# Moving the low halves of twenty weight units from GpSimd to VectorE, and reordering the work around them

## The chip, the cores and the metric

The kernel runs on one NeuronCore of a Trainium2 chip. The metric is the device time of one execution in microseconds; the median of several runs counts. The engines are called as the profile calls them: PE (TensorE), DVE (VectorE), ACT (ScalarE), POOL (GpSimd) and SP (SyncE, which issues the DMAs).

## What is computed

The reference is a two-layer transformer backbone over 512 latent tokens and 256 context tokens of width 1024. What matters here is the MLP behind each attention layer, its modulated input and its gated output:

```python
def squared_relu_mlp(h, w_in, w_out):
    return jnp.square(jax.nn.relu(h @ w_in)) @ w_out
...
    ml = jnp.split((c_act @ w_mod[i] + b_mod[i])[:, None, :], 6, axis=-1)
    ...
    xl = xl + ml[5] * squared_relu_mlp(modulate(xl, norm_mlp_g[i], ml[3], ml[4]), w_mlp_in[i], w_mlp_out[i])
    if not last:
        ...
        xc = xc + mc[5] * squared_relu_mlp(modulate(xc, norm_mlp_g[i], mc[3], mc[4]), w_mlp_in[i], w_mlp_out[i])
```

`w_in` is 1024 x 4096 and `w_out` 4096 x 1024, all in float32. The first MLP works on all 768 tokens, the second on the 512 latent ones.

## The kernel before

**Three matmuls for one.** Every operand of a float32 product is split into a high half (`w_hi`, `h_hi`, `hidh`: the value rounded to the matmul's format) and a low half (what is left: `w_lo`, `h_lo`, `hidl`). A product is three matmuls, lines 2109 to 2111: low by high, high by low, high by high.

**Weight units.** The weights come from DRAM in units of 128 x 1024, by SP, into four `raw` slots. For each unit ACT writes the high half (`high_u`, line 949, or `high_sum`, line 964) and POOL the low half in four pieces of 256 columns (`low`, line 744, `w_lo <- raw, w_hi`). PE waits for `lo_made`, a count of finished units in their order; SP reloads a raw slot when the low half that frees it is made (`FREED`).

**The first MLP.** It goes through the 4096 hidden columns in 8 blocks of 512. Block 0 is computed directly. Blocks 1 to 7 split both operands in 2 x 2 parts and use seven products p0 to p6 instead of eight (24 PE matmuls of 384 tokens each), with sums of parts as operands. For the weights, POOL's `summed` (line 770) makes four sums a block: S1 `w_sum = a21 + a22`, S2 `a21 = a11 - a21`, S3 `a11 = w_sum - a11`, S4 `w_sum = a12 - a11`. Products 1 and 3 use S1 and S4 from the one `w_sum` buffer, product 2 uses S3, product 4 uses S2. For the tokens DVE makes t1 to t4 once, at the end of block 0 (`differ`, `join`, `less`), ACT their high halves (`turn_high`, line 971) and DVE their low halves (`turn_low`, line 1681). POOL may start S1 of block 1 when the first `turn_low` is done, because t1 and `w_sum` share memory.

After its seven products, a block's hidden values are finished in quarters on ACT and DVE (`copy`, line 1007, which takes product 0, 1 or 2 out of PSUM; `joined`, line 1768; `quarter_high`, lines 1015 to 1019; `low(q)`, line 1773). PE product 2 waits for the first `copy`; in ACT's queue this copy stands behind `high_sum(b, 3)`, which needs S4. Then PE does the second matrix (`second`): four units of 48 matmuls, two output tiles a unit; the first two column chunks of tile 0 and 1 need quarters 0 and 1, the third chunk needs quarters 2 and 3. DVE adds each finished tile onto the residual (`add_tile`, line 1660).

**Modulation.** DVE also computes late rows of the modulation product (`mod_step`, line 1439, eight steps a row group, fed by SP through a ring of four slots; then `acc_hi`, `acc_lo`), PE sums them over the partitions (`mod_mm`, lines 2150 and 2151), and DVE reads the result out (`extract_late`). Groups 10 and 11 of these fall in the second MLP's first pass: eight units for the hidden values (i = 0 to 7), eight for the output (i = 8 to 15).

Every engine runs its own list in program order; the order is written out by hand.

Of the kernel before, what the change touches and what calls it, by code (L numbers as in the profile page):

```python
# [58 lines left out]
MOD_LATE = {6: (10, (4, 5)), 7: (10, (6, 7)), 8: (11, (0, 1)), 9: (11, (2, 3)), 11: (11, range(4, 8))}  # L59
# [15 lines left out]
def _sources():  # L75

    src, freed = {}, {}
    for b in range(BLOCKS):
        w, r = block_first(b), block_raw(b)
        n = 8 if b == 0 else 0  # L80
        if b:
            src.update({w: r, w + 1: None, w + 2: r, w + 3: None, w + 4: r + 1, w + 5: r + 2, w + 6: r + 3})
            freed.update({r: w + 2, r + 1: w + 4, r + 2: w + 5, r + 3: w + 6})
            w, r, n = w + 7, r + 4, 4 if b < 6 else 0
        for i in range(n):
            src[w + i], freed[r + i] = r + i, w + i
    for i in range(8):
        src[LAST_W + i], freed[LAST_R + i] = LAST_R + i, LAST_W + i
    return src, freed
# [40 lines left out]
def build(nc, t):  # L130

    ctx = ExitStack()
    with ctx:
# [200 lines left out]
        tf_made = sem("tf_made")  # L334
        t_hi = sem("t_hi")
# [400 lines left out]
        def _(pool):  # L736
# [28 lines left out]
            def first_mlp():  # L765
# [9 lines left out]
                for b in range(1, BLOCKS):  # L775
                    w, r, n = M0 + block_first(b), M0 + block_raw(b), 4 * (b - 1)
                    a11, a21, a12, a22 = (raw[:, (r + j) % SLOTS] for j in range(4))

                    def raw_here(j):
                        pool.wait_ge(raw_in[(r + j) % SLOTS], 16 * ((r + j) // SLOTS + 1))  # L780

                    def outer_sums():
                        raw_here(1)
                        raw_here(3)
                        if b == 1:
                            pool.wait_ge(t_lo, 1)
                        else:
                            pool.wait_ge(lo_made, M0 + block_first(b - 1) + 4)
                        summed(w_sum, a21, a22, ALU.add)
                        raw_here(0)  # L790
                        pool.wait_ge(w_sums, n + 1)
                        summed(a21, a11, a21, ALU.subtract)

                    if b < 7:
                        outer_sums()
                    low(w, 4)
                    pool.wait_ge(w_sums, n + 2)
                    pool.wait_ge(lo_made, w + 1)
                    summed(a11, w_sum, a11, ALU.subtract)
                    low(w + 1, 4)  # L800
                    raw_here(2)
                    pool.wait_ge(w_sums, n + 3)
                    pool.wait_ge(lo_made, w + 2)
                    summed(w_sum, a12, a11, ALU.subtract)
                    for j in range(2, 11 if b < 6 else 7):
                        low(w + j, 4)
# [136 lines left out]
        def _(act):  # L943
# [23 lines left out]
            def first_mlp():  # L967

                def turn_high(j, dst, src):
                    act.wait_ge(tf_made, (2, 3, 2, 4)[j])  # L970
                    nc.scalar.activation(dst, src, ACT.Copy).then_inc(t_hi, 1)
# [22 lines left out]
                turn_high(3, t4h[:], t4f[:])  # L994
# [6 lines left out]
                next_block(1)  # L1001
                for b in range(1, BLOCKS):
# [421 lines left out]
        def _(dve):  # L1424
# [252 lines left out]
            def first_mlp():  # L1677
# [8 lines left out]
                def differ(dst, spare, j0, tok0, j1, tok1):  # L1686
                    tt(dst, half_f(j0, 0, tok0), half_f(j1, 0, tok1), op=ALU.subtract).then_inc(dsteps, 1)
                    st.n = st.n + 1
                    st.wait(tt(spare, half_f(j0, 1, tok0), half_f(j1, 1, tok1), op=ALU.subtract))

                def join(dst, other):
# [16 lines left out]
                join(t1f[:], t4f[:])  # L1708
# [33 lines left out]
                join(t3f[:], t4f[:])  # L1742
                add_tile(0, 1)
                less(t2f[:], t1f[:], 1, 1, H1)
                join(t2f[:], half_f(1, 1, H1))
                add_tile(0, 2)
                turn_low(0, h_lo[:, 0:4, H1], t1f[:], h_hi[:, 0:4, H1])
# [10 lines left out]
                for b in range(1, BLOCKS):  # L1758
# [15 lines left out]

                    early = 4 if b < 5 else 6
# [8 lines left out]
                    low(1)  # L1784
                    if b == 6:
                        extract_late(c, 4)
                    joined(1, 5, 2)
                    low(2)
                    low(3)
                    if b < 5:  # L1790
                        for m in range(8):
                            add_tile(b, m)
                            if m < 2:
                                steps(c, range(6 + m, 7 + m))
                            if m == 4:
                                extract_late(c, 0)
                    elif b == 5:
                        add_tile(b, 0)
                        add_tile(b, 1)
                        extract_late(c, 0)  # L1800
# [20 lines left out]
            def mlp():  # L1821
                u0 = FIRST["mlp1"]

                def blk(b, first, last):
                    for i in range(12 if last else 16):
# [3 lines left out]
                        else:  # L1829
                            if first and i in (8, 12):  # L1830
                                dve.wait_ge(mod_done, PE_MODS + i // 4 + 9)
# [3 lines left out]
                        if first:  # L1835
# [3 lines left out]
                            elif i == 7:  # L1839
                                extract_late(10, 6)  # L1840
                            elif i in (8, 9):
                                for k in range(4 * i - 32, 4 * i - 28):
                                    mod_step(11, k)
                            elif i == 10:
                                extract_late(11, 6)
# [258 lines left out]
        def _(pe):  # L2104
# [269 lines left out]
            def mlp(layer=1):  # L2374
# [3 lines left out]
                def blk(b, first, last):  # L2378
                    for i in range(12 if last else 16):
# [24 lines left out]
                        if first and i in (7, 10):  # L2404
                            mod_mm(10 if i == 7 else 11, 6)
# [574 lines left out]
```

## Time and profile before

| | us |
|---|---|
| median of 3 runs | 1601.85 (1601.6 to 1603.73) |
| profiled execution, its own time | 1603.09 |
| its span, first to last instruction | 1601.3 |
| PE busy / DVE busy / ACT busy / POOL busy | 1573.3 / 894.1 / 604.7 / 910.0 |
| PE's longest wait in the first MLP | 4.6, for POOL's `w_lo` |

The busy times are sums over the whole span. A product starts on PE only when the last of its weights, tokens and PSUM banks is there, so a wait of PE names the one that came last, and the row of that engine shows what it waited for in turn.

### The profile page before, as it was taken

The numbers are of one execution on the slowest core, as the hardware profiler recorded it, in microseconds if no ns is written. First come the engines' busy times: TensorE is split into PE (matmuls) and PEld (weight loads), VectorE is DVE, ScalarE is ACT, GpSimd is POOL, SyncE is SP. The second block draws the span as 40 slices with busy tenths as digits, with TensorE's granted clock in tenths as the row PEclk, the third lists the DMA queues.
The fourth block names the chain that finished last, engine by engine and source line by source line (L and its number), as shares of the span: only waits on it lengthen the run. The fifth ranks groups of instructions, "written<-read, shape, count | busy, mean of one in ns | idle before, by whom it ended". The sixth has DMA issues, their size and how long they took to land.

```text
span 1601.3 us, 24059 instructions
## 1 busy us (share of the span) xinstructions
PE 1573.3 (98%) x9272; PEld 1408.7 (88%) x9272; DVE 894.1 (56%) x1364; ACT 604.7 (38%) x1009; POOL 910.0 (57%) x1103
## 2 busy tenths in 40 slices
PE   8999999999899999999999999999999999999998
PEld 5889988988899999999998888878889878888887
DVE  4696457347845656647556746049965753232234
ACT  4422456325252342442542511248853412222222
POOL 2443475326677768768762656354415865555562
PEclk9999999999999999999999999999999999999999
DMA  8574212212042232333352223110003332323221
GB/s 350 197 268 153 93 41 100 80 48 85 27 157 81 80 119 82 116 115 123 105 182 82 91 78 96 66 43 1 1 12 130 129 126 93 105 92 101 83 93 53
DMA packets 50348, 163.15 MB, mean 102 GB/s; under 512 B 6336, under 2 KB 8768, under 8 KB 46656
## 3 DMA queue, kind: packets, MB, share of 16 engines
q1 hardware_dynamic: 50240, 161.68, 29.4%
q8 instruction: 71, 1.16, 0.3%
q14 instruction: 37, 0.30, 0.1%
HBM read 158.78 MB, written 2.10 MB: 100 GB/s over the span
## 4 chain that ended last, share of the span: by engine, by line
PE 86%; DVE 6%; POOL 2%; issue 2%; DMA 2%; ACT 1%; SPq 0%; POOLq 0%; DVEq 0%; ACTq 0%
PE ps L2109 24%; PE ps L2110 24%; PE ps L2111 24%; PE ps L2748 3%; PE ps L2710 2%; PE ps L2737 1%; PE ps L2615 1%; POOL w_lo L744 1%; PE ps L2603 1%; PE ps L2643 1%; PE ps L2427 1%; DVE mod_acc L1439 1%; DMA mod_big<-w_mod_dram 1%; DVE h L1562 1%; DMA raw<-units_dram 1%
## 5 line engine op out<-in xcount | busy, mean ns | idle before, releaser
L744 POOL TENSOR_TENSOR w_lo<-raw,w_hi 128x256 fp32r<-128x256 f32 x776 | 639.4, 856 | 492.4 <-ACT w_hi L949 362.0
L2109 PE MATMUL ps<-h,w_hi 128*128 128x512 f32 (+2 forms) x1016 | 358.0, 352 | 7.2 <-POOL w_lo L744 4.6
L2110 PE MATMUL ps<-h,w_lo 128*128 128x512 f32 (+2 forms) x1016 | 355.3, 350 | 0.0
L2111 PE MATMUL ps<-h,w_hi 128*128 128x512 f32 (+2 forms) x1016 | 355.0, 349 | 0.0
L2109 PEld LDWEIGHTS ps<-h,w_hi 128*128 128x128 f32 x1016 | 192.2, 189 | 32.3 <-issue 9.1
L2111 PEld LDWEIGHTS ps<-h,w_hi 128*128 128x128 f32 x1016 | 192.0, 189 | 17.1
L2110 PEld LDWEIGHTS ps<-h,w_lo 128*128 128x128 f32 x1016 | 192.2, 189 | 16.4
L1660 DVE SCALAR_TENSOR_TENSOR xl<-ps,mods,xl 128x384 f32<-128x384 f32 (+2 forms) x144 | 73.0, 539 | 210.8 <-PE ps L2111 209.0
L949 ACT ACTIVATE w_hi<-raw 128x1024 fp32r<-128x1024 f32 x120 | 126.4, 1054 | 113.2 <-PE ps L2111 107.7
L2109 PE MATMUL ps<-hidl,w_hi 128*128 128x384 f32 (+2 forms) x448 | 150.4, 336 | 2.5 <-DVE hidl L1704 1.5
L2110 PE MATMUL ps<-hidh,w_lo 128*128 128x384 f32 (+2 forms) x448 | 149.8, 334 | 0.0
L2111 PE MATMUL ps<-hidh,w_hi 128*128 128x384 f32 (+2 forms) x448 | 149.8, 334 | 0.0
L1439 DVE SCALAR_TENSOR_TENSOR mod_acc<-mod_ring,cact,mod_acc 128x512 f32<-128x512 f32 x112 | 105.7, 964 | 17.1 <-DVE mod_acc L1439 8.4
L2109 PE MATMUL ps<-hid_lo,w_hi 128*128 128x512 f32 (+1 forms) x288 | 105.6, 367 | 0.8 <-DVE hid_lo L1674 0.8
L2110 PE MATMUL ps<-hid_hi,w_lo 128*128 128x512 f32 (+1 forms) x288 | 105.3, 366 | 0.0
L2111 PE MATMUL ps<-hid_hi,w_hi 128*128 128x512 f32 (+1 forms) x288 | 105.3, 366 | 0.0
L956 ACT ACTIVATE w_hi<-raw 128x1024 fp32r<-128x1024 f32 x60 | 63.4, 1057 | 108.5 <-PE ps L2111 108.5
L2109 PEld LDWEIGHTS ps<-hidl,w_hi 128*128 128x128 f32 x448 | 84.1, 188 | 4.3 <-DVE hidl L1704 1.8
L2110 PEld LDWEIGHTS ps<-hidh,w_lo 128*128 128x128 f32 x448 | 84.1, 188 | 1.3 <-issue 0.2
L2111 PEld LDWEIGHTS ps<-hidh,w_hi 128*128 128x128 f32 x448 | 84.1, 188 | 0.6
L1670 DVE TENSOR_TENSOR tmp_b<-tmp_a 128x512 f32<-128x512 f32 x32 | 28.0, 875 | 81.7 <-ACT tmp_a L1141 81.1
L770 POOL TENSOR_TENSOR w_sum<-raw 128x256 f32<-128x256 f32 x52 | 48.6, 965 | 26.2 <-issue 17.9
(301 smaller groups left out, 3181.1 us busy)
## 6 DMA issues: line engine op xcount, KB each, us to landing
raw<-units_dram SPq DMA_DIRECT2D x187, 512.0 KB, 3.4
mod_ring<-w_mod_dram SPq DMA_DIRECT2D x96, 256.0 KB, 3.9
mod_big<-w_mod_dram SPq DMA_DIRECT2D x16, 1024.0 KB, 10.2
mod_late<-w_mod_dram SPq DMA_DIRECT2D x8, 1024.0 KB, 8.1
xl<-x_dram SPq DMA_DIRECT2D x2, 2048.0 KB, 8.3
bias<-bias_dram SPq DMA_DIRECT2D x8, 384.0 KB, 3.7
xc<-ctx_dram SPq DMA_DIRECT2D x2, 1024.0 KB, 10.4
out_dram<-out_t SPq DMA_DIRECT2D x16, 128.0 KB, 1.8
```

Source lines behind the costliest of these rows:

```text
L744: ins = nc.gpsimd.tensor_tensor(w_lo[:, s, sl], src[:, sl], w_hi[:, s, sl].bitcast(F32), op=ALU.subtract)
L770: ins = nc.gpsimd.tensor_tensor(dst[:, sl], a[:, sl], b[:, sl], op=op)
L949: nc.scalar.activation(w_hi[:, u % SLOTS], raw[:, r % SLOTS], ACT.Copy).then_inc(hi_made, 1)
L956: nc.scalar.activation(w_hi[:, u % SLOTS], raw[:, r % SLOTS], ACT.Copy).then_inc(hi_made, 1)
L1439: ins = V.scalar_tensor_tensor(out=mod_acc[:, v], in0=w, scalar=cact[:, k, v:v + 1], in1=mod_acc[:, v], op0=ALU.mult, op1=ALU.add)
L1660: ins = V.scalar_tensor_tensor(out=x, in0=ps[:, 2 * par + bank, cols], scalar=gate(layer, m, v, i), in1=x, op0=ALU.mult, op1=ALU.add)
L1670: ins = tt(tmp_b[:, i % 2, 0:n], tmp_a[:, i % 2, 0:n], tmp_a[:, i % 2, 0:n], op=ALU.mult)
L2109: mm(out, a[0], b[1], start=start, stop=False, skip_group_check=onto)
L2110: mm(out, a[1], b[0], start=False, stop=False, skip_group_check=onto)
L2111: return mm(out, a[0], b[0], start=False, stop=stop, skip_group_check=onto)
L2710: return mm(scores_ps(n)[:, TOK * i + keys.start:TOK * i + keys.stop], a[p][64 * i:64 * i + 64, tok], b[p][64 * i:64 * i + 64, keys], star ...
L2748: ins = mm(out_ps, v1[:, c, P * h:P * h + P], aturn[m % 2][:, c], start=c == 0, stop=c == NT - 1)
```

## The change

Three things change.

1. At the end of block 0, DVE and ACT take their steps in another order: the low half of t1 comes second instead of after the other sums, ACT's `turn_high(0)` waits for the first join alone (and for a new count `t_read`, that the parts it overwrites were read), and ACT's high half of t4 stands behind the first three weight high halves of block 1.
2. In blocks 1 to 7, POOL makes the low half of product 2's weights before S4 instead of behind it. In blocks 1 to 5 the low halves of the four second-matrix units are made by DVE (`weight_low`), whole units of 1024 columns, between its other steps.
3. In the second MLP's first pass, PE sums group 10 after unit 8 instead of after unit 7 and group 11 after unit 11 instead of after unit 10; DVE reads them out at i = 8 and 12; the steps of group 11 are spread over i = 8, 9, 10 as 2, 3, 3 instead of 4, 4; the ring loads move with them.

```diff
-MOD_LATE = {6: (10, (4, 5)), 7: (10, (6, 7)), 8: (11, (0, 1)), 9: (11, (2, 3)), 11: (11, range(4, 8))}
+MOD_LATE = {6: (10, (4, 5)), 7: (10, (6, 7)), 8: (11, range(4)), 12: (11, range(4, 8))}
...
-            freed.update({r: w + 2, r + 1: w + 4, r + 2: w + 5, r + 3: w + 6})
+            freed.update({r: w + 3, r + 1: w + 4, r + 2: w + 5, r + 3: w + 6})
...
                     low(w + 1, 4)
+                    low(w + 2, 4)
                     raw_here(2)
                     pool.wait_ge(w_sums, n + 3)
                     pool.wait_ge(lo_made, w + 2)
                     summed(w_sum, a12, a11, ALU.subtract)
-                    for j in range(2, 11 if b < 6 else 7):
+                    for j in range(3, 7):
                         low(w + j, 4)
...
-                    act.wait_ge(tf_made, (2, 3, 2, 4)[j])
+                    act.wait_ge(tf_made, (1, 3, 2, 4)[j])
+                    if j == 0:
+                        act.wait_ge(t_read, 4)
...
-                turn_high(3, t4h[:], t4f[:])
...
                 next_block(1)
+                turn_high(3, t4h[:], t4f[:])
...
+                    def weight_low(j):
+                        if b < 6:
+                            u = M0 + block_first(b) + 7 + j
+                            dve.wait_ge(hi_made, u + 1)
+                            dve.wait_ge(lo_made, u)
+                            tt(w_lo[:, u % SLOTS], raw[:, raw_of(u) % SLOTS], w_hi[:, u % SLOTS].bitcast(F32),
+                               op=ALU.subtract).then_inc(lo_made, 1)
...
                     low(1)
+                    weight_low(0)
...
                     joined(1, 5, 2)
                     low(2)
+                    weight_low(1)
                     low(3)
+                    weight_low(2)
...
                             if first and i in (8, 12):
+                                extract_late(i // 4 + 8, 6)
...
-                        if first and i in (7, 10):
-                            mod_mm(10 if i == 7 else 11, 6)
+                        if first and i in (8, 11):
+                            mod_mm(10 if i == 8 else 11, 6)
```

The fourth `weight_low` of a block follows the last modulation step of the row group behind the second `add_tile` (in block 5, the second `add_tile` itself).

POOL's list from the end of block 6 to the end of the first MLP. `w_lo<-w_sum` are the low halves for products 1 and 3, `raw<-w_sum,raw` is S3, `w_sum<-raw` is S4. Before:

```order
L744 TENSOR_TENSOR w_lo<-raw,w_hi 128x256 x16
L770 TENSOR_TENSOR raw<-w_sum,raw 128x256 x4
L744 TENSOR_TENSOR w_lo<-w_sum,w_hi 128x256 x4
L770 TENSOR_TENSOR w_sum<-raw 128x256 x4
L744 TENSOR_TENSOR w_lo<-raw,w_hi 128x256 x4
L744 TENSOR_TENSOR w_lo<-w_sum,w_hi 128x256 x4
L744 TENSOR_TENSOR w_lo<-raw,w_hi 128x256 x60
```

Now:

```order
L745 TENSOR_TENSOR w_lo<-raw,w_hi 128x256 x16
L771 TENSOR_TENSOR raw<-w_sum,raw 128x256 x4
L745 TENSOR_TENSOR w_lo<-w_sum,w_hi 128x256 x4
L745 TENSOR_TENSOR w_lo<-raw,w_hi 128x256 x4
L771 TENSOR_TENSOR w_sum<-raw 128x256 x4
L745 TENSOR_TENSOR w_lo<-w_sum,w_hi 128x256 x4
L745 TENSOR_TENSOR w_lo<-raw,w_hi 128x256 x60
```

S4 of block 7 moved behind the low half of product 2's weights; in blocks 1 to 6 the same pair is swapped.

DVE's list at the end of block 1's products, from the low half of quarter 0 to the first output tile. `hidl<-ps,hidh` are the quarters' low halves, `ps<-ps,hidl_f` are the joins. Before:

```order
L1773 TENSOR_TENSOR hidl<-ps,hidh 128x2x384
L1768 TENSOR_TENSOR ps<-ps,hidl_f 128x2x384
L1439 SCALAR_TENSOR_TENSOR mod_acc<-mod_ring,cact,mod_acc 128x512 x2
L1773 TENSOR_TENSOR hidl<-ps,hidh 128x2x384
L1768 TENSOR_TENSOR ps<-ps,hidl_f 128x2x384
L1773 TENSOR_TENSOR hidl<-ps,hidh 128x2x384 x2
L1660 SCALAR_TENSOR_TENSOR xl<-ps,mods,xl 128x384
```

Now:

```order
L1778 TENSOR_TENSOR hidl<-ps,hidh 128x2x384
L1773 TENSOR_TENSOR ps<-ps,hidl_f 128x2x384
L1443 SCALAR_TENSOR_TENSOR mod_acc<-mod_ring,cact,mod_acc 128x512 x2
L1778 TENSOR_TENSOR hidl<-ps,hidh 128x2x384
L1785 TENSOR_TENSOR w_lo<-raw,w_hi 128x1024
L1773 TENSOR_TENSOR ps<-ps,hidl_f 128x2x384
L1778 TENSOR_TENSOR hidl<-ps,hidh 128x2x384
L1785 TENSOR_TENSOR w_lo<-raw,w_hi 128x1024
L1778 TENSOR_TENSOR hidl<-ps,hidh 128x2x384
L1785 TENSOR_TENSOR w_lo<-raw,w_hi 128x1024
L1664 SCALAR_TENSOR_TENSOR xl<-ps,mods,xl 128x384
```

Three whole-unit low halves now stand between the quarters, the first of them ahead of quarter 2's join.

ACT's list from the last hidden tile of block 0 to block 1's first copy (`hidl_f<-ps`). Before:

```order
L983 ACTIVATE hidh<-hidl_f 128x768
L971 ACTIVATE h<-t1f 128x4x384
L971 ACTIVATE t2h<-t2f 128x1536
L971 ACTIVATE t3h<-t3f 128x1536
L971 ACTIVATE t4h<-t4f 128x1536
L949 ACTIVATE w_hi<-raw 128x1024
L964 ACTIVATE w_hi<-w_sum 128x1024
L964 ACTIVATE w_hi<-raw 128x1024
L964 ACTIVATE w_hi<-w_sum 128x1024
L1007 ACTIVATE hidl_f<-ps 128x2x384
```

Now:

```order
L987 ACTIVATE hidh<-hidl_f 128x768
L975 ACTIVATE h<-t1f 128x4x384
L975 ACTIVATE t2h<-t2f 128x1536
L975 ACTIVATE t3h<-t3f 128x1536
L951 ACTIVATE w_hi<-raw 128x1024
L966 ACTIVATE w_hi<-w_sum 128x1024
L966 ACTIVATE w_hi<-raw 128x1024
L975 ACTIVATE t4h<-t4f 128x1536
L966 ACTIVATE w_hi<-w_sum 128x1024
L1011 ACTIVATE hidl_f<-ps 128x2x384
```

The high half of t4 moved behind the high halves for products 0, 1 and 2.

## Rows read from the trace of the kernel before

**Rows 1.** The page: the span, and PE's busy time, share and instructions.

```profile
span 1601.3 us, 24059 instructions
...
PE 1573.3 (98%) x9272; PEld 1408.7 (88%) x9272; DVE 894.1 (56%) x1364; ACT 604.7 (38%) x1009; POOL 910.0 (57%) x1103
```

**Rows 2.** Waits of PE in the first MLP: total, times, longest.

```profile
PE ps L2109 <- POOL w_lo L744: 4.6, 1, 4.6
```

**Rows 3.** Timeline of PE in block 1: start, duration, instruction, idle before.

```profile
433.40 0.34 PE L2111 MATMUL ps<-h,w_hi 128*128 128x384 f32 x1
...
438.31 0.66 PE L2109 MATMUL ps<-h,w_hi 128*128 128x384 f32 x1 [4.56 <-POOL w_lo L744]
...
445.26 0.34 PE L2109 MATMUL ps<-t2l,w_hi 128*128 128x384 f32 x1
```

**Rows 4.** Windows: length, busy PE PEld DVE ACT POOL, PEclk, DMA.

```profile
437.40:444.20 6.80, 5.89 (x18) 5.93 (x19) 3.37 (x4) 1.90 (x3) 6.63 (x8) 0.50 0.00 0
...
500.30:563.66 63.36, 63.36 (x365) 63.18 (x365) 37.35 (x54) 22.84 (x26) 47.62 (x60) 1.00 0.30 100
```

**Rows 5.** Timeline of POOL from block 0 into block 1.

```profile
385.05 20.75 POOL L744 TENSOR_TENSOR w_lo<-raw,w_hi 128x256 fp32r<-128x256 f32 x16 [7.14 <-ACT w_hi L949]
412.85 4.33 POOL L770 TENSOR_TENSOR w_sum<-raw 128x256 f32<-128x256 f32 x4 [7.05 <-DVE h L1681]
...
426.41 2.83 POOL L744 TENSOR_TENSOR w_lo<-raw,w_hi 128x256 fp32r<-128x256 f32 x4 [4.67 <-ACT w_hi L949]
429.38 4.52 POOL L770 TENSOR_TENSOR raw<-w_sum,raw 128x256 f32<-128x256 f32 x4
```

**Rows 6.** Timeline of DVE and ACT in the same stretch.

```profile
410.93 1.75 DVE L1681 TENSOR_TENSOR h<-t1f,h 128x1536 fp32r<-128x1536 f32 x1
...
425.29 1.04 ACT L949 ACTIVATE w_hi<-raw 128x1024 fp32r<-128x1024 f32 x1
...
443.26 0.79 ACT L1007 ACTIVATE hidl_f<-ps 128x768 f32<-128x768 f32 x1
```

**Rows 7.** Timeline of DVE (low half of quarter 3, third output tile) and PE, block 2.

```profile
532.70 0.96 DVE L1773 TENSOR_TENSOR hidl<-ps,hidh 128x768 fp32r<-128x768 f32 x1 [2.37 <-ACT hidh L1019]
...
544.48 0.86 DVE L1660 SCALAR_TENSOR_TENSOR xl<-ps,mods,xl 128x384 f32<-128x384 f32 x2
...
534.62 0.33 PE L2109 MATMUL ps<-hidl,w_hi 128*128 128x384 f32 x1
```

**Rows 8.** Timeline of DVE, block 6.

```profile
779.00 1.21 DVE L1725 TENSOR_TENSOR w_sum<-raw 128x1024 f32<-128x1024 f32 x1
```

**Rows 9.** Timeline of POOL, start of block 3.

```profile
540.16 4.99 POOL L770 TENSOR_TENSOR w_sum<-raw 128x256 f32<-128x256 f32 x4 [3.66 <-issue]
...
565.06 3.64 POOL L744 TENSOR_TENSOR w_lo<-w_sum,w_hi 128x256 fp32r<-128x256 f32 x4 [2.63 <-ACT w_hi L964]
```

**Rows 10.** Timeline of POOL, ACT and PE, start of block 7.

```profile
787.32 2.82 POOL L770 TENSOR_TENSOR w_sum<-raw 128x256 f32<-128x256 f32 x4 [0.17 <-POOL w_lo L744]
790.10 3.02 POOL L744 TENSOR_TENSOR w_lo<-raw,w_hi 128x256 fp32r<-128x256 f32 x4
...
787.67 1.05 ACT L964 ACTIVATE w_hi<-raw 128x1024 fp32r<-128x1024 f32 x1
...
790.99 1.05 ACT L964 ACTIVATE w_hi<-w_sum 128x1024 fp32r<-128x1024 f32 x1
...
793.17 0.45 PE L2109 MATMUL ps<-t2l,w_hi 128*128 128x384 f32 x1
```

**Rows 11.** Timeline of PE, behind block 7.

```profile
820.95 0.44 PE L2109 MATMUL ps<-h,w_hi 128*128 128x384 f32 x1 [0.43 <-DVE h L1773]
```

**Rows 12.** Timeline of PE, second MLP, first pass.

```profile
1280.39 0.47 PE L2150 MATMUL ps<-acc_lo,ones 128*128 128x512 f32 x1 [1.23 <-DVE acc_lo L1449]
...
1286.64 0.50 PE L2109 MATMUL ps<-hid_lo,w_hi 128*128 128x512 f32 x1 [0.76 <-DVE hid_lo L1674]
...
1299.72 0.48 PE L2150 MATMUL ps<-acc_lo,ones 128*128 128x512 f32 x1 [1.19 <-DVE acc_lo L1449]
```

More of the change, by code:

```diff
@@ L334, in build @@
         tf_made = sem("tf_made")
+        t_read = sem("t_read")
         t_hi = sem("t_hi")
@@ L1686, in differ, with join @@
                 def differ(dst, spare, j0, tok0, j1, tok1):
[L1687 to L1691, printed above, removed]
+                    tt(dst, half_f(j0, 0, tok0), half_f(j1, 0, tok1), op=ALU.subtract).then_inc(t_read, 1)
+                    tt(spare, half_f(j0, 1, tok0), half_f(j1, 1, tok1), op=ALU.subtract).then_inc(t_read, 1)
+                def join(dst, other, reads=None):
+                    if reads:
+                        dve.wait_ge(t_read, reads)
                     tt(dst, dst, other, op=ALU.add).then_inc(tf_made, 1)
@@ L1707, in first_mlp @@
                 differ(t1f[:], t4f[:], 0, H1, 0, H0)
-                join(t1f[:], t4f[:])
+                join(t1f[:], t4f[:], 2)
                 first_square(0)
@@ L1741, in first_mlp @@
                 add_tile(0, 0)
-                join(t3f[:], t4f[:])
+                less(t2f[:], t1f[:], 1, 1, H1)
+                turn_low(0, h_lo[:, 0:4, H1], t1f[:], h_hi[:, 0:4, H1])
                 add_tile(0, 1)
-                less(t2f[:], t1f[:], 1, 1, H1)
+                join(t3f[:], t4f[:], 4)
+                add_tile(0, 2)
                 join(t2f[:], half_f(1, 1, H1))
-                add_tile(0, 2)
-                turn_low(0, h_lo[:, 0:4, H1], t1f[:], h_hi[:, 0:4, H1])
                 add_tile(0, 3)
@@ L1794, in first_mlp @@
                                 steps(c, range(6 + m, 7 + m))
+                            if m == 1:
+                                weight_low(3)
                             if m == 4:
@@ L1799, in first_mlp @@
                         add_tile(b, 1)
+                        weight_low(3)
                         extract_late(c, 0)
@@ L1838, in blk @@
                                 mod_step(10, 2 * i - 3)
[L1839 to L1845, printed above, removed]
+                            for k in {8: (0, 1), 9: (2, 3, 4), 10: (5, 6, 7)}.get(i, ()):
+                                mod_step(11, k)
                 blk(0, True, False)
```

## The prediction

> **What bounds the kernel now.** First the busy shares [rows 1]: PE works 1573.3 of 1601.3 us, so work moved between POOL, DVE and ACT counts only where PE waits, or where a new wait of PE appears. Next the waits of PE in the first MLP [rows 2]: one is large, 4.6 us for a low half of POOL. The timeline puts it into block 1 [rows 3]: product 0's last matmul starts at 433.40, product 1's first at 438.31, product 2's at 445.26. Undisturbed, block 2 runs 365 matmuls in 63.36 us at granted clock 1.00 [rows 4], 0.174 each, 4.17 for a product. Block 1's product 0 thus began at 433.40 - 23 x 0.174 = 429.4, and product 2, due at 429.4 + 8.3 = 437.7, was 7.5 late. About 2.5 of that is clock: from 437.4 to 444.2 the granted clock is 0.50 (1.2 instead of 2.4 GHz) [rows 4], after PE had stood still, and the 17 steps between matmul starts from 438.8 to 444.2 take 0.32 instead of 0.174.
>
> Why POOL was late [rows 5, 6]: S1 started at 412.85, behind t1's low half on DVE (410.93 + 1.75), and product 0's low half at 426.41, behind ACT's high half of 425.29, which stood in ACT's queue behind t4.
>
> **Part 1, block 1: both waits go, another ends last.** POOL's last low half of block 0 ends at 385.05 + 20.75 = 405.8; the raw unit it frees is needed for S1 and comes 3.66 later (that gap in rows 9), at 409.5. t1's low half, now ahead of the joins of t3 and t2 and of two output tiles, should end near 407 (estimate: the first output tile ends near 403.5, then two steps of 1.75 [rows 6]). So S1 starts at 409.5 instead of 412.85. A POOL group of four pieces takes 2.83 when DVE is quiet and up to 4.52 beside it [rows 5]: S1 4.3 to 413.8, S2 4.4 to 418.2, product 0's low half to 421.3, S3 4.5 to 425.8, product 1's low half to 428.7, then, swapped ahead, product 2's to 432.2, and S4 4.3 to 436.5. Products 0 and 1 no longer wait. Product 2 does: it needs product 0 copied out of PSUM, and in ACT's queue that copy stands behind the high half of S4: 436.5 + 1.04 + 0.79 [rows 6] = 438.4. Product 2 starts at 438.5 instead of 445.26: **gain 6.75**, 4.25 without the clock's part. Bounds: with POOL quiet it starts when due, 437.7 (7.5); with every group at 4.52 and 1.5 later, 5.2.
>
> **Part 2, low halves on DVE, twenty in five blocks.** A DVE operation of this form and size took 1.21 [rows 8], one start every 1.14 or so (estimate, overlapped). POOL is quiet then, having given these units up. The first stands ahead of quarter 2's join, so quarters 2 and 3 come 1.14 later through ACT. Quarter 3's low half ended at 532.70 + 0.96 = 533.66, and PE used it at 534.62 [rows 7]: the cover is 0.96 less some 0.15 for the restart. New end 534.80, PE starts near 534.9 and loses a tenth more: 0.35 a block, **loss 1.8 in five** (0 if the DVE operation overlaps more, 3 at 0.6 a block). The second and third low halves lie in DVE's idle time, hidden by the 8.3 us that PE spends on a unit.
>
> The fourth stands behind the last modulation step, ahead of the third output tile, which started at 544.48 [rows 7]; it ends near 545.0 (POOL no longer slows the steps before it). POOL's fourth ended 3.66 before 540.16 [rows 9], at 536.5. Queued behind it: SP's load of the unit that S1 of the next block needs, the ring loads behind that load, and POOL's whole chain. Block 3: S1 from 548.7; six groups of 2.83 (S1, S2, low, S3, low, low) with small gaps to 566.0; S4 beside DVE's steps 3.64 [rows 9] to 569.7; high half and copy to 571.5. Product 2 is due at 563.66 [rows 4] + 8.3 = 572.0, with the 0.35 above 572.3. It fits with 0.8 to spare: no cost, but where 8 us of slack were, under one is left.
>
> **Part 3, the swap of S4 in block 7.** Here the swap hurts [rows 10]. Before, S4 ran at 787.32 to 790.14, while ACT was busy with block 6's last quarters; the high half of product 2's weights was made at 787.67 to 788.72, between two quarters, and POOL's low half came after. Now POOL, done with product 1's low half at 787.2, must wait for 788.72, makes product 2's low half to 791.6, and only then S4, beside DVE's steps: 3.64 to 4.99 [rows 9], I take 3.9, to 795.5. ACT's high half of S4 moves from 790.99 to 795.5, the copy behind it ends at 797.2, and product 2 starts at 797.25 instead of 793.17 [rows 10]: **loss 4.1**, PE standing still for about as long. Bounds: 3.0 (S4 at 2.82) and 5.2 (at 4.99). The Trainium skill ("SBUF — State Buffer", Who interferes with whom) says that a VectorE operation with two SBUF inputs and a GpSimd one that reads SBUF exclude each other for a whole instruction, the later one blocking fully. By that S4 lies at the upper row and the loss is 5.2; by the row of 3.64 beside the same kind of steps it is 3.8. The rows decide for something between.
>
> Behind block 7 the 0.77 step before 820.95 [rows 11] should go, since the data that DVE waited for then has more lead: **gain 0.6** (0 if not).
>
> **Part 4, second MLP** [rows 12]. The wait of 1.23 before group 10's sum is taken from in front of unit 8, but unit 8's last step still waits for the same low half (1286.64), now about 2 us; the sum's two matmuls follow and cost 0.5. Group 11's wait of 1.19 shrinks to some 0.2, since one DVE step less lies behind the last output tile. **Gain 0.6** (-0.5 to 1.2; two ring loads issue later, behind a raw load, and could hold DVE).
>
> **Sum.** 6.75 - 1.8 - 4.1 + 0.6 + 0.6 = 2.05 against the profiled execution's 1603.09, with the clock unhurt in block 7. But 1603.09 lies 1.24 above the median, and the runs shown spread by 2.1, near the 2.5 that the low clock costs: I read the median as executions that kept their clock in block 1. For these the first term is 4.25 and the sum -0.45: 1601.85 + 0.45 = 1602.3.
>
> **The rivals.**
> *Faster: block 7 does not bite* (S4's high half or the copy finds another way round, or POOL is ahead). For it: POOL's block 7 list is short. Against: the order rows, where S4 is plainly behind a low half that needs 788.72. Time: 1602.3 - 4.1 = 1598.2, and 1596.4 if the lows on DVE are hidden too. Chance 0.15.
> *Slower: POOL's late start reaches PE in blocks 2 to 6.* Place: S1 behind the fourth low half; it decides once the chain is 0.8 later than I have it. For it: one group at 4.99 instead of 2.83 suffices. Against: in that stretch DVE mostly adds tiles out of PSUM, beside which groups stay at 2.83. Price: 2.2 late leaves 1.4 a block, 7 in five: 1609. At 1.5 late, 1606. Chance 0.12.
> *Slower: the clock falls in block 7 as it did in block 1.* The idle of 4.56 was followed by half clock, the 1.23 of rows 12 was not; the new 4.1 is nearer the former. The Trainium skill ("TensorE: Matmul & The Clock Gate", Part 1: The HAM clock gate) says too that an idle PE falls to 1.2 GHz; the trace agrees, 0.50 behind 4.56 us. Price 2.5: 1604.8. Chance 0.13; the spread of the runs shown lets me think that one execution has it and another not.
> *The forecast*, the wait moves from block 1 to block 7: 0.6, own range 1600 to 1604.
>
> **How the numbers follow.** A measurement of this kernel tells about 0.2%, 3.2 us, from no change: faster is under 1598.6, slower over 1605.05. The first rival gives faster 0.15; the second, with the upper end of the third, slower 0.17; the rest, 0.68, is the same. The range leaves about a tenth at each end: 1597.5 to 1606.
>
> **What would show it.** Right: block 1's wait for POOL gone, a step of about 1 before product 2; a step of 4 to 5 before block 7's product 2, behind ACT's copy; steps of a few tenths at quarter 3 in blocks 1 to 5; S1 of blocks 2 to 5 some 8 later against PE. Wrong: waits at product 2 of blocks 2 to 6, low halves on DVE well over 1.2, or block 7 without a step.

## The result, and the profile after

The changed kernel takes 1609.75 us (median of 6 runs, 1608.24 to 1610.23); the kernel before, run beside it, 1602.32 (6 runs, 1601.6 to 1603.73). The ratio is 1.0047, 95% interval 1.0036 to 1.0058: slower by 7.4 us, where 1602.3 was forecast. The profiled execution took 1609.88, its span is 1607.9.

The page of the changed kernel, span and busy times (against [rows 1]):

```profile
span 1607.9 us, 24021 instructions
...
PE 1574.1 (98%) x9272; PEld 1409.7 (88%) x9272; DVE 910.4 (57%) x1384; ACT 603.9 (38%) x1009; POOL 843.9 (52%) x1023
```

POOL gave up 66 us of work and DVE took 16; PE's work is the same. The waits of PE in the first MLP (against [rows 2]): total, times, longest.

```profile
PE ps L2124 <- ACT hidl_f L1011: 5.2, 1, 5.2
PE ps L2124 <- ACT h_f L1011: 4.3, 1, 4.3
```

The wait for POOL is gone, and two for ACT's copies stand in its place. `hidl_f` is the copy of product 0 in block 1, `h_f` the same in block 7. The timeline of PE (against [rows 3], [rows 10] and [rows 12]):

```profile
435.68 0.34 PE L2126 MATMUL ps<-h,w_hi 128*128 128x384 f32 x1
...
441.24 0.66 PE L2124 MATMUL ps<-t2l,w_hi 128*128 128x384 f32 x1 [5.22 <-ACT hidl_f L1011]
...
797.71 0.41 PE L2124 MATMUL ps<-t2l,w_hi 128*128 128x384 f32 x1 [4.32 <-ACT h_f L1011]
...
1288.84 0.50 PE L2124 MATMUL ps<-hid_lo,w_hi 128*128 128x512 f32 x1 [0.25 <-DVE hid_lo L1678]
1291.98 0.50 PE L2124 MATMUL ps<-hid_lo,w_hi 128*128 128x512 f32 x1 [2.17 <-DVE hid_lo L1678]
1311.84 0.48 PE L2165 MATMUL ps<-acc_lo,ones 128*128 128x512 f32 x1 [0.47 <-DVE acc_lo L1453]
```

Product 1 no longer waits in block 1; product 2 does, for as long. Behind each long wait the granted clock falls. Windows of the changed kernel (columns as in [rows 4]):

```profile
439.92:446.75 6.83, 5.51 (x17) 5.54 (x18) 0.00 (x0) 3.77 (x5) 6.28 (x10) 0.50 0.34 115
...
798.32:801.74 3.42, 3.42 (x12) 3.42 (x12) 0.00 (x0) 1.83 (x3) 3.42 (x6) 0.50 0.24 68
1293.26:1296.67 3.41, 3.41 (x10) 2.64 (x9) 3.10 (x5) 0.84 (x1) 2.50 (x4) 0.50 0.23 89
```

The column before the last two is the clock: 0.50, 1.2 GHz, in three places. The kernel before had it in one of them ([rows 4]), and once more in its first microseconds, where the changed kernel's execution did not. Window of the kernel before, near the start:

```profile
20.96:27.78 6.82, 6.82 (x26) 2.80 (x27) 1.61 (x8) 3.40 (x6) 2.97 (x5) 0.50 1.02 414
```

**Where the time went.** Both kernels issue 9272 matmuls, so the same one can be looked up in both timelines. The table gives its start after, less its start before:

| the matmul | before | after | difference |
|---|---|---|---|
| in product 0 of block 1 | 430.45 | 428.57 | -1.88 |
| first of product 2, block 1 | 445.26 | 441.24 | -4.02 |
| 18th of product 2, block 1 | 448.21 | 446.80 | -1.42 |
| behind quarter 3, block 5 | 724.88 | 725.19 | +0.31 |
| first of product 2, block 7 | 793.17 | 797.71 | +4.54 |
| 15th of product 2, block 7 | 795.73 | 801.78 | +6.05 |
| behind block 7 | 820.95 | 826.39 | +5.44 |
| first of unit 12, second MLP | 1305.75 | 1312.39 | +6.64 |

The first 1.9 belong to the startup of the execution before, not to the change: matmuls that start at 100 to 400 us, ahead of anything that was changed, are already 1.9 to 2.0 apart. From there: block 1 costs 0.5 (-1.88 to -1.42), the five quarters 1.7, block 7 5.7, behind it 0.6 comes back, the second MLP costs 1.2: 8.5 in all between these two executions, against 7.4 between the medians. Each kernel has one trace here, so how far the other executions share each of these terms is not shown.

### The profile page after: what moved, and what is told of

Read it like the earlier page. It is cut to its first block, busy times and chain, and to the rows that moved or that the text cites. A ratio compares the mean times of both kernels' runs of the same rounds, so it can differ in the third digit from the quotient of the medians.

```text
span 1607.9 us, 24021 instructions
## 1 busy us (share of the span) xinstructions
PE 1574.1 (98%) x9272; PEld 1409.7 (88%) x9272; DVE 910.4 (57%) x1384; ACT 603.9 (38%) x1009; POOL 843.9 (52%) x1023
## 4 chain that ended last, share of the span: by engine, by line
PE 79%; DVE 7%; POOL 4%; ACT 4%; issue 3%; DMA 2%; SPq 1%; POOLq 0%; DVEq 0%; ACTq 0%
PE ps L2124 22%; PE ps L2125 22%; PE ps L2126 22%; PE ps L2763 3%; POOL w_lo L745 2%; PE ps L2725 2%; DMA raw<-units_dram 2%; PE ps L2752 1%; PE ps L2630 1%; PE ps L2618 1%; PE ps L2658 1%; ACT ps L1021 1%; ACT ps L1019 1%; DVE ps L1773 1%; POOL w_sum L771 1%
## 5 line engine op out<-in xcount | busy, mean ns | idle before, releaser
L745 POOL TENSOR_TENSOR w_lo<-raw,w_hi 128x256 fp32r<-128x256 f32 x696 | 578.4, 865 | 452.1 <-ACT w_hi L951 323.1
L1443 DVE SCALAR_TENSOR_TENSOR mod_acc<-mod_ring,cact,mod_acc 128x512 f32<-128x512 f32 x112 | 100.6, 918 | 34.8 <-DMA mod_ring<-w_mod_dram 24.1
```

The source lines that it names most:

```text
L745: ins = nc.gpsimd.tensor_tensor(w_lo[:, s, sl], src[:, sl], w_hi[:, s, sl].bitcast(F32), op=ALU.subtract)
L1443: ins = V.scalar_tensor_tensor(out=mod_acc[:, v], in0=w, scalar=cact[:, k, v:v + 1], in1=mod_acc[:, v], op0=ALU.mult, op1=ALU.add)
```

## The experiments

Unless it is said otherwise, each is the changed kernel with one edit, and times are medians against its 1609.75. The kernel before, run beside them, had medians of 1601.3 to 1601.7, which is 0.6 to 1.0 under the 1602.32 beside the changed kernel; each gain below may be smaller by that much.

**Block 7's order put back.**

```diff
-                    low(w + 2, 4)
+                    if b < 7:
+                        low(w + 2, 4)
...
                     summed(w_sum, a12, a11, ALU.subtract)
+                    if b == 7:
+                        low(w + 2, 4)
```

> The changed kernel, but in block 7 S4 stands ahead of the low half of product 2's weights again, as before the change. Theory (the swap makes product 2 of block 7 late, and the clock falls behind that wait): the step of 4.65 at product 2 shrinks to about 0.45 and the stretch of half clock after 798.3 goes, so 4.2 + 1.5 = 5.7 less than the changed kernel's 1609.75: about 1604. If the clock falls there anyway: 4.2 less, 1605.5. Rival (the loss sits with the low halves on DVE, and block 7 is late for their sake): no change, 1609.8.

Measured: 1603.94 (11 runs, 1602.76 to 1605.29), ratio to before 1.0014 (1.0005 to 1.0023). 5.8 gained, 5.2 when each is taken against the kernel before beside it. PE's product 2 in block 7 follows product 1 with a step of 0.45, as in the kernel before:

```profile
793.93 0.45 PE L2127 MATMUL ps<-t2l,w_hi 128*128 128x384 f32 x1
```

The row shows no idle time, and no half clock follows in this execution. The swap in block 7 alone was most of the net loss.

**The first low half on DVE behind quarter 2's join.**

```diff
-                    weight_low(0)
...
                     joined(1, 5, 2)
+                    weight_low(0)
```

> The changed kernel, but the first of DVE's four low halves of second-matrix weights stands behind the join of quarter 2 instead of ahead of it, so that it lies in DVE's wait for quarter 2's high half. Theory (that one operation delays quarters 2 and 3): the five steps of 0.39 at the third chunk of the second matrix in blocks 1 to 5 go to about 0.2, and 5 x 0.34 = 1.7 is gained: about 1608. Rival (the four low halves together, or POOL's later start, make the step): no change, 1609.8.

Measured: 1607.18 (5 runs, 1606.45 to 1611.6), 2.6 gained. In the changed kernel PE stops in blocks 1 to 5 where quarter 3 is first needed; block 1's row, with 0.39 between the two starts instead of the usual 0.17:

```profile
469.68 0.34 PE L2126 MATMUL ps<-hidh,w_hi 128*128 128x384 f32 x1
470.06 0.45 PE L2124 MATMUL ps<-hidl,w_hi 128*128 128x384 f32 x1
```

In this run's trace the five steps of 0.39 are gone; block 1's now reads

```profile
469.74 0.33 PE L2126 MATMUL ps<-hidh,w_hi 128*128 128x384 f32 x1
469.92 0.33 PE L2124 MATMUL ps<-hidl,w_hi 128*128 128x384 f32 x1
```

with 0.18 between starts, as everywhere. The same unit of work costs PE something or nothing by standing on one side or the other of one join.

**Product 1 computed twice.**

```diff
+                        if p == 1 and b in (1, 7):
+                            product(b, p, False)
                         product(b, p)
```

(`False` leaves out the count at the end.)

> The changed kernel, but PE computes product 1 of blocks 1 and 7 twice, the second time into the same place with the same result: 24 more matmuls, 4.17 us, in each of the two long waits ahead of product 2 (5.2 and 4.3). The output is the same. Theory (the half clock behind each wait is the price of PE's standing still): product 2 starts when it did, the clock stays at 1.00 in both places, and 2.5 + 1.5 = 4.0 is gained although PE does 8.3 us more work: about 1605.8. Rival (the clock falls for some other reason, or had nothing to do with the wait): no change or up to 0.5 slower, 1609.8 to 1610.3.

Measured: 1606.26 (6 runs, 1603.65 to 1606.85): 3.5 gained by 8.3 us more of work, 2.9 when each is taken against the kernel before beside it. The timeline of PE and the windows around the three former falls:

```profile
440.81 0.41 PE L2124 MATMUL ps<-t2l,w_hi 128*128 128x384 f32 x1 [1.12 <-ACT hidl_f L1011]
...
794.71 0.41 PE L2124 MATMUL ps<-t2l,w_hi 128*128 128x384 f32 x1 [0.20 <-ACT h_f L1011]
...
1287.34 0.50 PE L2124 MATMUL ps<-hid_lo,w_hi 128*128 128x512 f32 x1 [2.15 <-DVE hid_lo L1678]
```

```profile
435.00:446.75 11.75, 10.62 (x61) 10.33 (x61) 4.17 (x4) 5.86 (x7) 10.58 (x14) 1.00 0.19 57
789.50:801.74 12.24, 12.04 (x70) 11.75 (x70) 3.45 (x5) 6.11 (x7) 11.07 (x16) 1.00 0.31 97
1287.30:1296.67 9.37, 9.33 (x41) 7.72 (x42) 6.68 (x9) 2.12 (x2) 4.03 (x6) 1.00 0.51 168
```

Product 2 starts no sooner against the work around it, but at clock 1.00. Here the half clock is the price of standing still. The third window shows that it is not always charged: the same wait, 2.17 in the changed kernel and 2.15 here, was followed by 0.50 there and by 1.00 here.

**The second MLP as it was.** The edit undoes that part of the change:

```diff
-                        if first and i in (8, 11):
-                            mod_mm(10 if i == 8 else 11, 6)
+                        if first and i in (7, 10):
+                            mod_mm(10 if i == 7 else 11, 6)
```

and with it the read-outs, steps and loads.

> The changed kernel with the second MLP's first pass as it was before the change. Theory (without the fallen clock the rearrangement gains 0.5, by the trace the clock costs 1.6 of it): in executions whose clock fell there, 1.1 less, about 1608.6; with the clock unhurt in either, 0.5 more, 1610.3. Rival (the new order costs more than the trace of the changed kernel shows): 1607 or less.

Measured: 1609.14 (5 runs, 1607.99 to 1609.61), 0.6 less, inside what the runs spread, and the kernel before, beside it, was lower by 0.6 too: both stand at 1.0047 of it. This part is worth less than a microsecond either way, and the run does not say which way.

**Block 1's low half of product 2 on DVE, S4 directly behind product 1's on POOL.**

```diff
-                    low(w + 2, 4)
+                    if b > 1:
+                        low(w + 2, 4)
...
+                    if b == 1:
+                        pool.wait_ge(lo_made, w + 3)
                     for j in range(3, 7):
...
                 add_tile(0, 7)
+                u = M0 + block_first(1) + 2
+                dve.wait_ge(hi_made, u + 1)
+                dve.wait_ge(lo_made, u)
+                tt(w_lo[:, u % SLOTS], raw[:, raw_of(u) % SLOTS], w_hi[:, u % SLOTS].bitcast(F32),
+                   op=ALU.subtract).then_inc(lo_made, 1)
                 turn_low(3, t4l[:], t4f[:], t4h[:])
...
-                    high_sum(b, 3)
+                    if b > 1:
+                        high_sum(b, 3)
                     copy(0, 0, 2)
+                    if b == 1:
+                        high_sum(b, 3)
```

> The changed kernel, but in block 1 the low half of product 2's weights is made by DVE (one operation of 1024 columns, about 1.2 us, ahead of t4's low half), POOL goes on to S4 directly, and ACT copies product 0 out of PSUM ahead of S4's high half. Theory (product 2 of block 1 is late because POOL's seven groups there take 32 us where I had 27, and the copy waits for the last of them): product 2 starts when due, near 435.9 instead of 441.24, the clock does not fall, product 3 finds its weights within half a microsecond: 5.3 + 2.5 = 7.8 less than 1609.75, about 1602. Half of the gain, 1604.5, if S4's high half makes product 3 late by 2 to 3. Rival (product 2 is late for another reason, the copy or the token sums): no gain.

Measured: 1602.9 (11 runs, 1602.22 to 1604.81), 6.9 gained, ratio to before 1.0007 (0.9998 to 1.0016), which is no difference from the kernel before. Of block 1's waits this is left:

```profile
441.26 0.44 PE L2135 MATMUL ps<-h,w_hi 128*128 128x384 f32 x1 [0.82 <-POOL w_lo L745]
```

Product 3 waits 0.82; product 2 does not wait, and the clock stays up there.

**The second matrix's low halves back on POOL.**

```diff
-                    for j in range(3, 7):
+                    for j in range(3, 11 if b < 6 else 7):
...
-                        if b < 6:
+                        if False:
                             u = M0 + block_first(b) + 7 + j
```

> The changed kernel with the low halves of the second matrix's weights in blocks 1 to 5 back on POOL; the reorderings stay. Theory (moving them gains nothing anywhere and costs 0.34 a block through quarter 3): 1.7 less, about 1608; nothing changes at product 2 of blocks 2 to 6, and block 1's late product 2 stays. Rival (the move frees POOL and is what keeps blocks 2 to 6 without waits once the halves are swapped): slower, 1611 or more.

Measured: 1607.32 (5 runs, 1606.89 to 1608.85), 2.4 gained, about as much as by moving one of the four. No wait for POOL appears in blocks 2 to 6. Relieving POOL by 66 us bought nothing.

**Block 1's modulation steps behind S4.**

```diff
+                    if b == 1:
+                        dve.wait_ge(w_sums, 4)
                     steps(c, range(early))
```

> The changed kernel, but DVE begins block 1's modulation steps only when S4 of block 1 is made, so POOL's last two groups there run beside a quiet DVE. Theory (a POOL group takes 2.83 alone and 4.2 to 5.7 beside DVE's two-operand steps): the low half of product 2's weights and S4 shorten from 5.15 and 4.58 to about 3.5 and 2.83, product 2 of block 1 starts 3.4 earlier, and the wait left is about 2, so 3.4 is gained with the clock falling and up to 5.9 without: 1606.3 to 1603.8. Rival (the groups are long for another reason): no change, 1609.8, or slower where the late steps hold up the ring loads and what stands behind them.

Measured: 1605.95 (11 runs, 1603.92 to 1606.56), 3.8 gained. POOL's last two groups ahead of product 2, and product 2:

```profile
430.01 4.35 POOL L745 TENSOR_TENSOR w_lo<-raw,w_hi 128x256 fp32r<-128x256 f32 x4
434.31 2.80 POOL L771 TENSOR_TENSOR w_sum<-raw 128x256 f32<-128x256 f32 x4
...
439.04 0.66 PE L2126 MATMUL ps<-t2l,w_hi 128*128 128x384 f32 x1 [2.61 <-ACT hidl_f L1011]
```

S4 takes 2.80 instead of 4.58 beside a DVE that does nothing; the wait of 5.22 halves. The low half ahead of it was expected at 3.5 and still takes 4.35, beside the low half of t4 on DVE.

**The order of block 0's end alone.** This is the kernel before with that one part of the change.

```diff
                 add_tile(0, 0)
-                join(t3f[:], t4f[:])
-                add_tile(0, 1)
                 less(t2f[:], t1f[:], 1, 1, H1)
-                join(t2f[:], half_f(1, 1, H1))
-                add_tile(0, 2)
                 turn_low(0, h_lo[:, 0:4, H1], t1f[:], h_hi[:, 0:4, H1])
+                add_tile(0, 1)
+                join(t3f[:], t4f[:], 4)
+                add_tile(0, 2)
+                join(t2f[:], half_f(1, 1, H1))
                 add_tile(0, 3)
```

with ACT's order and the new count as in the change.

> The kernel before with the reordering of DVE and ACT at the end of block 0 alone: S4 stays ahead of product 2's low half, POOL keeps all low halves, the second MLP is unchanged. Theory (POOL's groups in block 1 are long beside DVE, so that the sooner start only shortens the wait): S4 ends near 434.9 and product 2's low half near 439.4 on the changed kernel's clock, so product 2 is 3.6 late with 2.5 of half clock behind it, 6.1 against the 7.5 of the kernel before: about 1.4 faster, 1600, or 1597.5 where the clock does not fall. Rival (the reordering itself removes block 1's waits, the swap brought them back): 7 faster, 1594.5.

Measured: 1598.75 (11 runs, 1596.65 to 1602.64), ratio to before 0.9987 (0.9978 to 0.9996): 2.6 faster. POOL's S4 and the low half behind it, and product 2 of block 1:

```profile
429.21 4.93 POOL L771 TENSOR_TENSOR w_sum<-raw 128x256 f32<-128x256 f32 x4 [0.17 <-POOL w_lo L745]
434.10 4.59 POOL L745 TENSOR_TENSOR w_lo<-raw,w_hi 128x256 fp32r<-128x256 f32 x4
...
438.79 0.41 PE L2113 MATMUL ps<-t2l,w_hi 128*128 128x384 f32 x1 [3.38 <-POOL w_lo L745]
```

The step before product 2 is 3.7, 3.5 over the usual 0.17, where 3.6 was expected; in this execution the clock stayed at 1.00 behind it, in others it need not have: the runs reach over 6 us. The swap in block 1 made the wait longer (5.22 against 3.38), since product 2 needs both groups either way, and behind the later of them there now stand a high half and a copy on ACT (1.06 and 0.79).

**The parts that help, together.** The order of block 0's end, block 1 as in the two runs above (low half on DVE, modulation steps behind S4), everything else in blocks 2 to 7 as before the change. In the second MLP:

```diff
+                        if first and i == 0:
+                            for k in range(3):
+                                mod_step(10, k)
...
-                            if 2 <= i < 6:
-                                mod_step(10, 2 * i - 4)
-                                mod_step(10, 2 * i - 3)
-                            elif i == 7:
+                            for k in {2: (3,), 3: (4,), 4: (5,), 5: (6, 7)}.get(i, ()):
+                                mod_step(10, k)
+                            if i == 7:
                                 extract_late(10, 6)
-                            elif i in (8, 9):
-                                for k in range(4 * i - 32, 4 * i - 28):
-                                    mod_step(11, k)
+                            for k in {7: (0, 1, 2), 8: (3, 4, 5), 9: (6, 7)}.get(i, ()):
+                                mod_step(11, k)
```

with `MOD_LATE` to suit (`{5: (10, (4, 5)), 6: (10, (6, 7)), 8: (11, range(4)), 10: (11, range(4, 8))}`).

> The reordering of block 0's end kept; block 1 as in the run with its low half on DVE and the modulation steps behind S4; all other blocks with S4 ahead of product 2's low half and the second matrix's low halves on POOL, as before the change; second MLP as before but with three of group 10's steps ahead of the first hidden tile, where DVE stood idle for 4.41, and group 11's steps spread 3, 3, 2 from one unit earlier. Theory: block 1's 7.5 to 7.8 gained against the kernel before, of the second MLP's three waits (1.23, 0.76 and 1.19) most: 3, and nothing lost elsewhere: 1602.3 - 7.6 - 3 = 1591.7. Rival (the order of block 1 only moves its wait to product 3): 1596; and 1599 if the second MLP gains nothing either.

Measured: 1592.96 (5 runs, 1591.71 to 1593.26), ratio to before 0.9943 (0.9929 to 0.9956). In the second MLP one wait is left, group 11's:

```profile
PE ps L2181 <- DVE acc_lo L1457: 0.8, 1, 0.8
```

**The same with group 11 summed one unit later.**

```diff
-                            if i == 10:
+                            if i == 11:
                                 extract_late(11, 6)
...
-                        if first and i in (7, 10):
-                            mod_mm(10 if i == 7 else 11, 6)
+                        if first and i in (7, 11):
+                            mod_mm(10 if i == 7 else 11, 6)
```

> The combined version, with the one part of the changed second MLP that the combined version lacked: PE sums group 11 after unit 11 instead of after unit 10, and DVE reads it out behind unit 11's tile. Theory (with DVE no longer behind, the later sum finds its operand made, and nothing waits in its place): the wait of 0.97 ahead of that sum goes, 1.0 less than the combined version's 1592.96: about 1592. Rival (the read-out, one unit later, delays the tile behind it, as in the changed kernel): no gain, 1593 or 1594.

Measured: 1591.21 (5 runs, 1590.57 to 1591.82), ratio to before 0.9933 (0.9920 to 0.9947): the fastest version, 10 us under the kernel before. Its page, and the longest waits of PE from block 1 to the end of the first MLP:

```profile
span 1588.8 us, 24061 instructions
...
PE 1566.0 (99%) x9272; PEld 1404.3 (88%) x9272; DVE 895.8 (56%) x1365; ACT 604.3 (38%) x1009; POOL 911.9 (57%) x1099
```

```profile
PE ps L2140 <- POOL w_lo L745: 1.0, 1, 1.0
PE ps L2140 <- DVE h L1787: 0.6, 1, 0.6
```

POOL works as long as it did before the change. PE's busy time is 7 us under that of the kernel before for the same 9272 matmuls; between its first microseconds and its last none of them ran at half clock.

## Why the prediction was wrong

**The step that failed is part 1, by the size of POOL's groups.** The path was the one foretold: S1 started when the raw unit came, products 0 and 1 did not wait, and product 2 waited for the copy behind S4's high half. Here are POOL's seven groups, then DVE beside the last of them:

```profile
407.21 5.23 POOL L771 TENSOR_TENSOR w_sum<-raw 128x256 f32<-128x256 f32 x4 [3.43 <-DMA raw<-units_dram]
412.58 4.17 POOL L771 TENSOR_TENSOR raw<-raw 128x256 f32<-128x256 f32 x4
416.70 4.34 POOL L745 TENSOR_TENSOR w_lo<-raw,w_hi 128x256 fp32r<-128x256 f32 x4
421.19 5.67 POOL L771 TENSOR_TENSOR raw<-w_sum,raw 128x256 f32<-128x256 f32 x4
426.82 2.84 POOL L745 TENSOR_TENSOR w_lo<-w_sum,w_hi 128x256 fp32r<-128x256 f32 x4
429.62 5.15 POOL L745 TENSOR_TENSOR w_lo<-raw,w_hi 128x256 fp32r<-128x256 f32 x4
434.73 4.58 POOL L771 TENSOR_TENSOR w_sum<-raw 128x256 f32<-128x256 f32 x4
```

```profile
429.37 1.91 DVE L1685 TENSOR_TENSOR t4l<-t4f,t4h 128x1536 fp32r<-128x1536 f32 x1 [0.37 <-ACT t4h L975]
431.20 1.83 DVE L1440 TENSOR_SCALAR mod_acc<-mod_ring,cact 128x512 f32<-128x512 f32 x2
433.25 2.07 DVE L1443 SCALAR_TENSOR_TENSOR mod_acc<-mod_ring,cact,mod_acc 128x512 f32<-128x512 f32 x2 [0.21 <-DVE mod_acc L1440]
```

I had 27.0 for the seven (4.3, 4.4, 3.1, 4.5, 2.9, 3.5, 4.3); they took 32.1. S1 started 0.4 sooner than I had it (407.21, and 1.9 of startup, against 409.5), so S4 ended 4.7 later, and product 2 at 441.24 instead of 436.6 on this execution's time (438.5 less 1.9). My durations were those of the same groups in their old places ([rows 5]). Started 3.7 and 6.3 us sooner, S1 and S3 fell beside other DVE steps and grew from 4.33 and 4.52 to 5.23 and 5.67; product 2's low half, in a place where I had no row, got 3.5 by guess and took 5.15. The upper bound was no bound. Every group at 4.52 was charged there as 1.5 later, but seven groups at 4.52 make 31.6, which is 4.6 more than 27.0 and near the 32.1 measured; and four groups took longer than 4.52. The run with the steps behind S4 shows the cause for S4 (2.80 against 4.58); for S1 and S3 it is read from the timelines alone. The run with the low half on DVE shows that this chain held product 2.

**The second step is the clock.** I took the half clock of block 1 as gone with the wait, counted that of block 7 as a rival with a chance of 0.13, and did not think of the second MLP. It fell in all three in the execution profiled. By the table above it took 2.6 in block 1 (-4.02 to -1.42), 1.5 in block 7 (4.54 to 6.05) and about 1.4 in the second MLP (seven steps of 0.43 between matmuls instead of 0.23). The run with product 1 twice gives back 2.9 to 3.5 of the first two's 4.1. So block 1, forecast at 4.25 to 6.75 gained, lost 0.5: product 2 started 2.1 sooner than before, and then ran its own 17 steps at half rate where before product 1 had done so. The price differs between executions. Block 7's wait of 4.3 is followed by half clock in all six traces that have it; the 40 steps from product 2's first matmul took 8.6 and 8.5 in the changed kernel and in the run with the second MLP as it was, 9.4 to 9.9 in the other four, and 7.0 at full clock in the run with product 1 twice. The second MLP's wait of 2.2 is followed by half clock in two of the seven traces that have it, so that its 1.4 need not stand in the medians.

I also read the median of before as executions that had kept their clock in block 1. The profiled execution's 1.2 over that median has another possible cause, the half clock at 20.96 to 27.78, which the runs do not separate from it. That the usual execution has a fall in block 1 is not shown by a trace; its mean granted clock over the later runs, 0.996 in most, is that of the run with block 1 mended, whose trace has one such stretch in block 7 and a shorter one at the start, while the two combined versions, with neither, have 0.997 to 0.999.

**Part 2 was right.** DVE's operation took 1.22, quarter 3's low half ended later by what I had worked out, and the step at PE was 0.39, 0.34 a block with its restart, 1.7 in five against 1.8. The two runs that take it away gain 2.6 and 2.4, or 2.0 and 1.4 when each is taken against the kernel before beside it. POOL's later start reached PE in no block from 2 to 6, as forecast.

**Part 3 was right in path and size.** The changed kernel's rows of POOL and ACT:

```profile
789.12 2.83 POOL L745 TENSOR_TENSOR w_lo<-raw,w_hi 128x256 fp32r<-128x256 f32 x4 [1.63 <-ACT w_hi L966]
791.90 3.87 POOL L771 TENSOR_TENSOR w_sum<-raw 128x256 f32<-128x256 f32 x4
...
795.81 1.06 ACT L966 ACTIVATE w_hi<-w_sum 128x1024 fp32r<-128x1024 f32 x1 [4.39 <-POOL w_sum L771]
796.77 0.79 ACT L1011 ACTIVATE h_f<-ps 128x768 f32<-128x768 f32 x1
```

S4 took 3.87 (3.9 forecast), product 2 was 4.2 later (0.31 to 4.54; 4.1 forecast). By the Trainium skill ("SBUF — State Buffer", Who interferes with whom), under which POOL would have been shut out for whole instructions, I had put it at 5.2; the trace stays below it. What was missing is the clock's 1.5, the third rival, priced at 2.5, which came true. The gap behind block 7 went as foretold (0.6).

**Part 4 was right but for the clock.** Unit 8's wait was 2.17 and 0.25 (about 2 forecast), group 11's 0.47 (0.2 forecast). Without the half clock the shift of 1.20 would be a gain of 0.2, against 0.6. What the change did not touch was the reason, that DVE was late by two steps a unit; three steps put into its idle 4.41 ahead of the first hidden tile, with group 11's steps begun a unit sooner, left one wait of 0.8, and the later sum took that away.

The sum with these sizes: -0.5 - 1.7 - 5.7 + 0.6 - 1.2 = -8.5. The first rival, that block 7 does not bite, is refuted by the trace; the second, that POOL's late start reaches PE in blocks 2 to 6, too.

## What to carry to other kernels

A step that is moved doesn't take its duration along: price it by the steps that it will stand beside, and where no row has that pair, let the upper end be well above the longest row, and add it up over the whole chain. In this kernel, where PE is busy 98% of the time, a wait costs its length and, where the clock falls behind it, 1.4 to 2.9 us more; so one wait traded for another of equal length gains nothing, and the trade can double the charge. Relief for an engine that PE does not wait for (POOL, outside block 1) was worth nothing as such; the one unit that moved with profit, together with a copy put ahead, was the one that stood in the chain ahead of PE's wait, and the place of an operation relative to one join decided whether it cost anything.

## What the runs showed of the hardware that was not expected

- A POOL group of four pieces took 2.80 to 2.84 beside an idle DVE, and also beside DVE's output tiles, which read one operand from PSUM (426.82 to 429.66, with tile adds at 427.74 to 429.00). Beside little more than one step of 1536 columns that reads two operands from SBUF it took about 1.4 more (4.17, 4.34), beside two of them 2.85 more (5.67). The Trainium skill ("SBUF — State Buffer", Who interferes with whom) says that a DVE operation with at most one SBUF input, outside the modes that use both port pairs, leaves GpSimd alone; for the output tiles the trace agrees. The two TENSOR_SCALAR steps that begin a group of the modulation, with one SBUF operand, did not go untouched: they took 1.83 beside POOL's low half (431.20) and 0.88 beside an idle POOL, in the run with the steps behind S4.
- How much POOL lost depended, in these traces, on the DVE step that it met. A single piece takes 0.73 beside a quiet DVE. One piece in the changed kernel beside the low half of t4 (429.37 to 431.28), and one of S4 beside the modulation steps:

```profile
429.62 2.25 POOL L745 TENSOR_TENSOR w_lo<-raw,w_hi 128x256 fp32r<-128x256 f32 x1
435.88 1.17 POOL L771 TENSOR_TENSOR w_sum<-raw 128x256 f32<-128x256 f32 x1
```

  The first ended 0.6 behind the DVE step, as if it had waited that step out. S4's four pieces took 4.58, while about four modulation steps ran, which take 0.74 each beside an idle POOL and 0.92 to 1.22 here: both engines are slowed, and less than if they took strict turns (2.8 for POOL alone and some 2.8 for the four steps, an estimate from these rows, make 5.6).
- The kernel gained about 3 us (2.9 to 3.5) by 8.3 us of useless matmuls in PE's waits.
- The length of a wait alone did not decide whether the clock fell: 2.17 was followed by 0.50 in one execution and by 1.00 in another, 2.61, in the run with the steps behind S4, by 0.50, and 3.38, in the run with block 0's order alone, by 1.00.
